# Reordering the first attention and giving two modulation tiles to TensorE in a two-block transformer kernel

## The reference

```
cond = silu(c)
mod = (cond @ ada_w[i] + ada_b[i])            # 6 * 1024 per layer
shift1, scale1, gate1, shift2, scale2, gate2 = split(mod, 6)
h = rmsnorm(x, norm1_g[i]) * (1 + scale1) + shift1
y = diff_attention(h, ...)                    # layer 0; layer 1 has grouped attention
x = x + gate1 * y
h = rmsnorm(x, norm2_g[i]) * (1 + scale2) + shift2
x = x + gate2 * swiglu(h, f_w_in[i], f_w_out[i])
```

```
p = softmax(q k^T)                # two maps c = 0, 1
w = p[0] - lam * p[1]
o = w @ v                         # 128 columns per head
o = rmsnorm(o, subln_g) * (1 - lam_init);  y = concat(o) @ w_o
```

## Time and profile before

| | us |
|---|---|
| median of 3 runs (1030.43 to 1033.04) | 1031.85 |
| the profiled execution | 1030.05 |
| its span | 1028.3 |
| PE busy | 983.7 (96%) |
| DVE busy | 740.3 (72%) |
| ACT busy | 541.2 (53%) |
| POOL busy | 70.5 (7%) |

### The profile page before, as it was taken

One profiled execution on the slowest core, in us unless ns is written; L12 is line 12 of the kernel. 1 busy time (PEld: TensorE's weight loads), 2 busy tenths in 40 slices (PEclk: granted clock), 3 DMA queues, 4 the chain that ended last, 5 costly groups with the idle time before them and its releaser, 6 DMA issues.

```text
span 1028.3 us, 13551 instructions
## 1 busy us (share of the span) xinstructions
PE 983.7 (96%) x5102; PEld 825.3 (80%) x5102; DVE 740.3 (72%) x1053; ACT 541.2 (53%) x874; POOL 70.5 (7%) x126
## 2 busy tenths in 40 slices
PE   2999799999999999999999999999999999999997
PEld 2887577788888777778888886888888789999986
DVE  5998888978888797877665557547653767777743
ACT  5366846544443486475444436565646374444442
POOL 3200222000000401010000002000000010000000
PEclk9899999999999999999999999999999999999999
DMA  9998166998889573459865564756444457566551
GB/s 339 368 362 298 46 205 223 353 314 290 275 300 386 176 221 116 144 181 301 254 189 190 187 185 128 248 173 192 141 126 143 130 184 222 183 185 184 186 183 41
DMA packets 126968, 219.89 MB, mean 214 GB/s; under 512 B 9235, under 2 KB 78088, under 8 KB 126904
## 3 DMA queue, kind: packets, MB, share of 16 engines
q1 hardware_dynamic: 125200, 215.52, 63.7%
q0 software_dynamic: 1088, 2.87, 0.9%
q10 hardware_dynamic: 616, 0.65, 0.2%
HBM read 217.96 MB, written 1.05 MB: 213 GB/s over the span
## 4 chain that ended last, share of the span: by engine, by line
PE 82%; DVE 8%; ACT 4%; DMA 2%; issue 2%; POOL 1%; SPq 0%; POOLq 0%; DVEq 0%; ACTq 0%
PE bank L1910 13%; PE bank L1912 13%; PE bank L1911 13%; PE bank L1923 5%; PE bank L1925 5%; PE bank L1924 5%; PE bank L2519 3%; PE bank L2521 3%; PE bank L2520 3%; DVE w_lo L1161 2%; PE bank L1973 2%; PE bank L1975 2%; PE bank L1974 2%; ACT w_hi L639 1%; DVE ada_acc L1191 1%
## 5 line engine op out<-in xcount | busy, mean ns | idle before, releaser
L1161 DVE TENSOR_TENSOR w_lo<-raw,w_hi 128x1024 fp32r<-128x1024 f32 x312 | 379.4, 1224 | 211.3 <-ACT w_hi L639 210.4
L639 ACT ACTIVATE w_hi<-raw 128x1024 fp32r<-128x1024 f32 x312 | 328.7, 1061 | 342.6 <-PE bank L1912 142.8
L1910 PE MATMUL bank<-w_hi,h_hi 128*128 128x512 f32 x608 | 243.6, 401 | 3.8 <-DVE w_lo L1161 3.8
L1912 PE MATMUL bank<-w_hi,h_lo 128*128 128x512 f32 x608 | 238.3, 392 | 0.0
L1911 PE MATMUL bank<-w_lo,h_hi 128*128 128x512 f32 x608 | 237.9, 391 | 0.0
L1910 PEld LDWEIGHTS bank<-w_hi,h_hi 128*128 128x128 f32 x608 | 114.9, 189 | 28.3 <-issue 5.8
L1912 PEld LDWEIGHTS bank<-w_hi,h_lo 128*128 128x128 f32 x608 | 114.7, 189 | 24.8
L1911 PEld LDWEIGHTS bank<-w_lo,h_hi 128*128 128x128 f32 x608 | 115.0, 189 | 23.2 <-issue 0.5
L2519 PE MATMUL bank<-h_hi,w_hi 128*128 128x256 f32 x320 | 90.7, 284 | 1.8 <-DVE conv_t L1838 1.8
L2521 PE MATMUL bank<-h_lo,w_hi 128*128 128x256 f32 x320 | 90.5, 283 | 0.0
L2520 PE MATMUL bank<-h_hi,w_lo 128*128 128x256 f32 x320 | 90.5, 283 | 0.0
(11 more groups left out here) (327 smaller groups left out, 1381.2 us busy)
## 6 DMA issues: line engine op xcount, KB each, us to landing
raw<-in_f_w_in SPq DMA_DIRECT2D x176, 256.0 KB
ada<-in_ada_w SPq DMA_DIRECT2D x86, 512.0 KB, 5.9
raw<-in_w_in SPq DMA_DIRECT2D x46, 512.0 KB
raw<-in_f_w_out SPq DMA_DIRECT2D x44, 512.0 KB
raw<-in_w_up SPq DMA_DIRECT2D x88, 256.0 KB
raw<-in_a_w_qkv SPq DMA_DIRECT2D x24, 512.0 KB
raw<-in_w_down SPq DMA_DIRECT2D x22, 512.0 KB
raw<-in_b_w_qkv SPq DMA_DIRECT2D x12, 512.0 KB
```

Of the source, the lines that this page charges most:

```text
L639: nc.scalar.activation(w_hi[:, m % SPL], raw[:, m % RAW], ACT.Copy).then_inc(hi_done, 1)
L1161: ve.tensor_tensor(w_lo[:, m % SPL], raw[:, m % RAW], w_hi[:, m % SPL].bitcast(F32), ALU.subtract).then_inc(lo_done, 1)
L1910: mm(o, hi, w_hi[:, s, k], start=(u == 0 and k == 0), stop=False)
L1912: last = mm(o, lo, w_hi[:, s, k], start=False, stop=(u == 3 and k == 1))
```

## The change

It touches the first attention and the tiles 24 to 39 of the modulation.

- Tiles 30 and 31 (the last two of vector 3) are no longer folded by DVE. PE multiplies them itself (`direct`, in halves of 4 matmuls of 64 columns, into bank 6), one half behind each of: scores 3, scores 4, scores 5 and scores 6. `add_folded` adds the accumulator of tiles 24 to 29 in two halves, behind scores 7 and behind `times_v_a(4)`. `reduce_vector(3)`, which stood in front of `pair_a(3)`, is gone. `take_vector(3)` moves from behind the last fold to the middle of the attention, in front of the weights of head 6.
- PE: `turn_a(0)` now stands ahead of the scores of head 2. `times_v_a` alternates between banks 5 and 7 and waits for the scaling of head h - 2 from head 2 on. Three of four pair transposes use bank 6.
- ACT: the copy of head h - 2 stands ahead of the exponentials of head h instead of behind. `split(28)` moves from ahead of the exponentials of head 2 to behind the squares of head 6.
- DVE: the weights of head 0 stand ahead of `low(26)`, `scale_a(7)` ahead of `low(29)`, and folds 32 to 39 stand at other tiles.
- SP: loads of modulation tiles move, and those of tiles 34 and 35 wait for PE (`direct_done`) instead of DVE.

```diff
-    after = dict(zip(range(16, 36), (8, 9, 10, 11, 12, 14, 15, 16, 18, 19, 20, 22, 23, 24, 26, 27, 28, 28, 29, 29)))
-    after.update({36: 31, 37: 31, 38: 31, 39: 31})
+    after = dict(zip(range(16, 30), (8, 9, 10, 11, 12, 14, 15, 16, 18, 19, 20, 22, 23, 24)))
+    after.update({32: 27, 33: 28, 34: 29, 35: 30, 36: 30, 37: 30, 38: 31, 39: 31})
...
-LOAD_BEFORE = {**FOLD_AFTER, 33: 29, 34: 30, 35: 31, 36: 32, 37: 32, 38: 33, 39: 33}
+LOAD_BEFORE = {**FOLD_AFTER, 30: 25, 31: 26, 32: 28, 33: 29, 34: 30, 35: 30, 36: 31, 37: 32, 38: 32, 39: 33}
+DIRECT = (30, 31)
...
-PAIR_BANKS_A = (5, 5, 4, 5)
-PV_BANKS_A = (5, 6, 7, 5, 6, 7, 6, 7)
+PAIR_BANKS_A = (6, 6, 4, 6)
+PV_BANKS_A = (5, 7, 5, 7, 5, 7, 5, 7)
+def folded(a):
+    return a - sum(d < a for d in DIRECT)
...
-                if a >= 18:
-                    sp.wait_ge(ada_done, a - ADA_SLOTS + 1)
+                if a - ADA_SLOTS in DIRECT:
+                    sp.wait_ge(direct_done, DIRECT.index(a - ADA_SLOTS) + 1)
+                elif a >= 18:
+                    sp.wait_ge(ada_done, folded(a - ADA_SLOTS + 1))
...
-                if AHEAD <= m < 23:
+                if AHEAD <= m < 22:
                     split(QKV_A + SPL + m)
...
             for i in range(NH + 3):
-                if 2 <= i < NH:
-                    exp_a(i)
                 if 2 <= i < NH + 2:
                     h = i - 2
                     act.wait_ge(wgt_t, h + 1)
                     nc.scalar.activation(wgtT[:, h % 2], ...)
+                if 2 <= i < NH:
+                    exp_a(i)
                 if i in (8, 9):
                     high_a(i - 8)
                 if i == 10:
+                    split(QKV_A + SPL + 22)
                     split(QKV_A + SPL + 23)
...
+                if m == 20:
+                    weight_a(0)
...
-            for i in range(1, NH + 1):
+            for i in range(2, NH + 1):
                 if 5 <= i <= 8:
                     scale_a(i - 5)
-                if 2 <= i < NH:
+                if i < NH:
                     max_a(i)
...
+                if i == 7:
+                    take_vector(3)
+                weight_a(i - 1)
...
             scale_a(6)
+            scale_a(7)
             low(QKV_A + SPL + 23)
-            scale_a(7)
             for m in range(WO_A, WO_A + 2):
                 low_a(2 + m - WO_A)
                 low(m + SPL)
-            take_vector(3)
...
+            def direct(a, q0):
+                g, k = divmod(a, 8)
+                tile, arrived, count = ada_tile(a)
+                pe.wait_ge(arrived, count)
+                for q in range(q0, q0 + 4):
+                    last = mm(bank[6][:, 64 * q:64 * q + 64], tile.rearrange("p a n -> p (a n)")[:, q * P:(q + 1) * P],
+                              cond[:, k:k + 1].to_broadcast([P, 64]), start=(a == DIRECT[0] and q == 0), stop=False)
+                if q0 == 4:
+                    last.then_inc(direct_done, 1)
+            def add_folded(g, q0):
+                pe.wait_ge(ada_done, folded(8 * (g + 1)))
+                for q in range(q0, q0 + 4):
+                    last = mm(bank[6][:, 64 * q:64 * q + 64], acc_of(g)[:, q * P:(q + 1) * P], ones[:, 0:64], start=False,
+                              stop=(q == 7))
...
-                if h >= 3:
-                    pe.wait_ge(o_ok, h - 2 if h < 6 else h - 1)
+                if h >= 2:
+                    pe.wait_ge(o_ok, h - 1)
...
+            turn_a(0)
+            scores_a(2)
+            scores_a(3)
+            direct(30, 0)
+            for h in range(6):
+                turn_a(h + 1)
+                if h == 5:
+                    pe.wait_ge(ada_col, COLUMN[3] + 1)
+                    pair_a(0)
+                times_v_a(h)
+                if h < 4:
+                    scores_a(h + 4)
+                if h == 0:
+                    direct(30, 4)
+                if h == 1:
+                    direct(31, 0)
+                if h == 2:
+                    direct(31, 4)
+                if h == 3:
+                    add_folded(3, 0)
+                if h == 4:
+                    add_folded(3, 4)
...
-            pe.wait_ge(o_ok, 7)
-            reduce_vector(3)
```

More of the change, by code:

```diff
@@ L1444, in max_a, with weight_a @@
                                  ALU.mult).then_inc(nmx_ok, 1)
+            def weight_a(h):
+                v_.wait_ge(exp_ok, h + 1)
+                r = stat[:, RDEN + 4 * h:RDEN + 4 * h + 4]
+                link(ve.reciprocal(r, stat[:, DEN + 4 * h:DEN + 4 * h + 4]))
+                link(ve.scalar_tensor_tensor(out=r[:, 2:4], in0=r[:, 2:4], scalar=neg_lam, in1=stat[:, DEN + 4 * h:DEN + 4 * h + 2],
+                                             op0=ALU.mult, op1=ALU.mult))
+                if h >= 2:
+                    v_.wait_ge(wgt_t, h - 1)
+                for t in range(T):
+                    last = ve.scalar_tensor_tensor(out=wgt[:, h % 2, t], in0=prob_a[:, h % 2, 1, t], scalar=r[:, 2 + t:3 + t],
+                                                   in1=prob_a[:, h % 2, 0, t], op0=ALU.mult, op1=ALU.add)
+                last.then_inc(wgt_ok, 1)
             for m in range(21):
@@ L2039, in reduce_vector @@
                 last.then_inc(ada_red, 1)
+            def direct(a, q0):
[8 more added lines that the diff above has]
+            def add_folded(g, q0):
+                pe.wait_ge(ada_done, folded(8 * (g + 1)))
+                for q in range(q0, q0 + 4):
+                    last = mm(bank[6][:, 64 * q:64 * q + 64], acc_of(g)[:, q * P:(q + 1) * P], ones[:, 0:64], start=False,
+                              stop=(q == 7))
+                if q0 == 4:
+                    last.then_inc(ada_red, 1)
             def reduce_after(m):
```

30 lines of the change are left out of this document (5 added, 25 removed).

## The result

| | before | changed |
|---|---|---|
| median, 16 runs each | 1030.88 (1028.65 to 1034.06) | 1035.51 (1032.79 to 1037.98) |
| the profiled execution | 1030.05 | 1035.49 |
| its span | 1028.3 | 1033.7 |

The ratio is 1.0040, with a 95% interval of 1.0029 to 1.0051: slower by 3.0 to 5.3 us. The forecast was 1034.5 us with a range of 1031.0 to 1037.5, and +2.65 us for the change. The sign and the place were right; the clock's rival came true on top.

What follows compares the result with a forecast made beforehand. The attention was taken to end bound by PE and the boundary by DVE; after the change the gate copy behind raw 33's load delays the first residual 2.65 us: 1031.85 + 2.65 = 1034.5 us, range 1031.0 to 1037.5.

Steps and rivals of the forecast that it cites:

- the clock's rival: Boundary: PE's 4.35 us gap in last_tall lowers its clock; 1 to 3.3 us on top of +2.65; chance 0.12.
- The heads: Attention's heads: direct matmuls fill PE's waits, rounds 3.38 us; early gain given back, heads end 0.25 us later.
- `low(28)`: End of the attention: DVE idles 3.55 us until ACT's late split(28), starting at 136.15; some 2.1 is paid back.
- `low_a(3)` and PE's wait: In last_tall PE does two of four tiles, then idles 4.35 us until low_a(3) at 148.95.
- DMA and gate copy: Boundary: raw 33 lands 5.93 us after issue, at 152.1; second gate copy done 153.7, first residual 2.65 us later.
- four signs that I had named for a wrong prediction: low(28) before 134 us, no PE gap in last_tall, first residual before 152, or granted clock dropping behind the gap.
- The sum: Whole kernel: the first residual's 2.65 us shift stays to the end, added to a median of 1031.85, giving 1034.5 us.
- within 0.3%: Whole kernel: time changes by less than 3.1 us either way; chance 0.54, against slower 0.39 and faster 0.07.
- A direct half cost: Heads: each direct half takes 1.72 us instead of 0.86, up to 1038.8 us in all; chance 0.04.
- The absorbed stall: DVE's queue before the first residual: stall vanishes, one fold saved, -1.3 us, 1030.5 us; chance 0.15.

Runs made afterwards that it cites:

- the filled tail: Changed kernel plus 17 unused 128x512 matmuls in PE's gap of last_tall, ahead of its wait for low_a(3); 1034.0 us, ratio 1.0032.
- the other three edits: Changed kernel with split(28) early, scale_a(7) behind fold 34, take_vector(3) behind head 6's weights, folds 36 and 37 behind low(31); 1028.78 us, ratio 0.9985.

## Why the prediction was right, and where not

- **The heads.** Turn of head 1 forecast at 4.62 behind T0, measured at 4.51. Rounds 3.38, measured 3.45: a direct half paces at 0.95 (109.19 to 110.14) and not at the 0.86 of the reduction. Turn 6 forecast at 22.12, measured at 22.16, released by DVE behind the take. Right. What I did not see is that the new order of heads would by itself have sped the rounds up to 2.66 to 3.35 us, so that the direct tiles, with the take of vector 3, cost 2.5 us there (19.67 against 22.16); with the take moved behind the weights of head 6 it is 0.8 (20.48). I compared them with the waits of the old order, which the change had already removed.
- **`low(28)`.** Forecast a wait of 3.55 and its start at 33.82 behind T0. Measured 3.44 and 35.02, of which 1.10 are the clock: 33.92. Right. Moving the split back gained 1.55 at `low_a(3)`, which agrees with the forecast that most of the stall is paid back by later waits.
- **`low_a(3)` and PE's wait.** Forecast 45.77 and a wait of 4.35; measured 46.12 in the filled tail without the clock's fall, 47.20 with it, and a wait of 4.10. Right within 0.35.
- **DMA and gate copy.** Forecast: raw 33 issued at 146.2, ready 5.93 later. SP's timeline of the changed kernel:

```profile
146.67 0.34 SPq L393 DMA_DIRECT2D ada<-in_ada_w  x1
147.42 1.90 SPq L371 DMA_DIRECT2D raw<-in_f_w_in  x4
```

  Issued at 147.42, which is 1.4 later from T0 than forecast, 1.1 of it by the clock; used at 152.92: 5.50 us. Without the fall the first residual depends on it, at 51.50 against the forecast 51.37. Right. The Trainium skill, "DMA: Bandwidth & Descriptors", section "Anatomy of one DMA — SWDGE (gpsimd) path", gave an estimated 3.2 us by its fit for the GpSimd path. The trace, where SyncE issues the load, does not agree; 5.50 is its number.
- **The clock was the step that failed.** I gave it a chance of 0.12, since the heads show a wait of 2.49 us without a fall, and took it to be settled by one wait's length. Of the four signs that I had named for a wrong prediction this one came, the other three did not. It fell behind the 4.10 us wait, cost 2.26 us (rival: 1 to 3.3), and made the gate half, not the DMA, last for the first residual, and PE last for the second. It fell in all five profiles in which PE waited 1.33 us or longer for a `low_a` in `last_tall`, and in none of the others. The Trainium skill, "TensorE: Matmul & The Clock Gate", section "HAM oscillation — how this bites in real kernels", says that idle gaps bring PE back to half clock. The trace agrees now: 0.50 granted from 151 to 156 us. No term of the sum, no rival held a fall near 125 us. It cost another 1.10 in three of the five profiles that have the same wait of about 1.5 us there; why not in the other two stays open.
- **The sum.** Forecast 2.65 at the boundary; 2.79 measured without the clock's falls at the second residual (52.83 - 50.04), 6.13 with both. The median moved by 4.6, the ratio says 3.0 to 5.3, which leaves 2.65 out. That the absolute forecast of 1034.5 is only 1.0 under the 1035.5 measured is in part luck: it was counted from the median of three runs, 1031.85, and the median of 16 is 1030.88. I had also given "within 0.3%" the larger chance, 0.54 against 0.39 for slower; 0.40% slower is what was measured. How many of the 16 executions had a fall can't be read, since only one was profiled, and the mean clock of a whole execution misses stretches, as at the start in three profiles (above). That the medians lie between the traces with and without the falls fits a mixture, which isn't shown.
- **The other rivals.** A direct half cost 0.09 above the row, not 0.86: out. The absorbed stall: out in the changed kernel. Its time, 1030.5 with a gain of 1.3, is close to what came when the split and the other three edits were undone, 1.57 us sooner at the second residual.

## What to carry to other kernels

Work that is put into an engine's waits is free only as long as those waits exist: if the same change also removes them, price the added work against the new order, and run each part alone. When an engine that bounds the next stage gets a wait (here `low(28)` behind the squares of head 6), follow its queue to the first result that PE needs, and put that result ahead of work that is due later: two folds ahead of `low_a(3)` moved it by 2.76 us. And where PE is given waits in a stretch that was full, count a fall of its clock as a likely case with a price, not as a rare one; a filler tells it apart from the wait itself.
